# Delta rounds of a two-block transformer kernel: filler work dealt out anew between the levels

## The reference, cut to what matters

```python
h = rms_norm(x, g_mix)
glu_a, glu_b, q, k, v, z, a_in, b_in, gate_a, gate_b = split_cols(h @ w_in, IN_SIZES)
c = depthwise_conv(glu_a * sigmoid(glu_b), conv_dw_w) + conv_dw_b      # 31 taps, 1024 channels
c = silu(layer_norm(c, ...));  y_conv = c @ w_conv_out
qkv = silu(depthwise_conv([q, k, v], qkv_conv_w))                      # 5 taps
# gated delta rule, forward and backward in time, 8 heads of 128, chunked:
lower = strictly lower part of (k_beta @ k.T) * decay
sol = triangular_solve(lower, [v * beta, k_beta * exp(g)], unit_diagonal=True)
v_new = u - w @ state;  o = q_dec @ state + qk @ v_new
state = state * exp(g_last) + k_tail.T @ v_new
y = sigmoid(gate_a) * y_conv + sigmoid(gate_b) * (norm(o_fwd + o_bwd) * silu(z)) @ w_delta_out
pl = rms_norm(p @ w_pl_proj, g_pl_proj)                                # gated in later
```

## Time and profile before

| | us |
|---|---|
| median of 3 runs (lowest, highest) | 2165.98 (2165.07, 2167.03) |
| the profiled execution's own time | 2168.76 |
| its span, first to last instruction | 2167.0 |
| PE busy in it | 2105.1 (97%), 14346 matmuls |
| DVE, ACT, POOL busy | 1210.3, 853.3, 154.5 |
| mean granted TensorE clock | 0.995 |

### The profile page before, as it was taken

How to read it: one execution, slowest core, us unless ns; L and a number is a source line. 1 busy time by engine, 2 the same in 40 slices (tenths; PEclk the granted TensorE clock), 3 DMA queues, 4 the chain that set the end, 5 groups by cost and what they waited for, 6 DMA issues and landing times.

```text
span 2167.0 us, 35176 instructions
## 1 busy us (share of the span) xinstructions
PE 2105.1 (97%) x14346; PEld 1747.7 (81%) x14346; DVE 1210.3 (56%) x1888; ACT 853.3 (39%) x1400; POOL 154.5 (7%) x134
## 2 busy tenths in 40 slices
PE   6999999999999999999999999999999999999998
PEld 5878777787878888888888888888897688888887
DVE  4789888798645554444433644443247835444323
ACT  4344655346674333333223533332243544322222
POOL 0100021002421010000000100000000110000000
PEclk9999999999999999999999999999999999999999
DMA  4242111122012342233323233233212122333321
GB/s 166 81 134 80 60 46 50 60 78 65 31 63 87 127 159 88 97 97 97 120 94 107 69 90 96 96 101 111 98 59 62 37 69 79 96 96 97 116 94 53
DMA packets 56173, 189.95 MB, mean 88 GB/s; under 512 B 6256, under 2 KB 8688, under 8 KB 56048
## 3 DMA queue, kind: packets, MB, share of 16 engines
q1 hardware_dynamic: 53168, 182.92, 26.4%
q10 hardware_dynamic: 2880, 5.24, 0.6%
HBM read 178.70 MB, written 9.44 MB: 87 GB/s over the span
## 4 chain that ended last, share of the span: by engine, by line
PE 65%; DVE 3%; ACT 1%; issue 0%; POOL 0%; DVEq 0%; ACTq 0%
PE pg L716 61%; PE pC L820 1%; DVE w_lo L2021 1%; PE pA L794 0%; PE pC L794 0%; PE pB L778 0%; ACT w_hi L1393 0%; PE pB L747 0%; DVE a_lo L2080 0%; DVE sml L2680 0%; DVE sm L2678 0%; PE pA L754 0%; DVE mo L2717 0%; PE pC L1308 0%; ACT a_hi L1953 0%
## 5 line engine op out<-in xcount | busy, mean ns | idle before, releaser
L716 PE MATMUL pg<-a_hi,w_hi 128*128 128x512 f32 (+1 forms) x1920 | 747.4, 389 | 14.2 <-ACT ptile L1483 4.4
L716 PE MATMUL pg<-a_lo,w_hi 128*128 128x512 f32 (+1 forms) x1920 | 739.9, 385 | 0.0
L716 PE MATMUL pg<-a_hi,w_lo 128*128 128x512 f32 (+1 forms) x1920 | 737.9, 384 | 0.0
L2021 DVE TENSOR_TENSOR w_lo<-w_raw,w_hi 128x1024 fp32r<-128x1024 f32 (+3 forms) x299 | 386.3, 1292 | 386.7 <-ACT w_hi L1393 386.0
L1393 ACT ACTIVATE w_hi<-w_raw 128x1024 fp32r<-128x1024 f32 (+3 forms) x299 | 329.6, 1102 | 646.0 <-PE pg L716 635.4
L716 PEld LDWEIGHTS pg<-a_hi,w_hi 128*128 128x128 f32 x1920 | 362.3, 189 | 91.3 <-issue 9.2
L716 PEld LDWEIGHTS pg<-a_hi,w_lo 128*128 128x128 f32 x1920 | 361.9, 188 | 68.9 <-issue 1.4
L716 PEld LDWEIGHTS pg<-a_lo,w_hi 128*128 128x128 f32 x1920 | 362.3, 189 | 67.8 <-issue 0.9
L716 PE MATMUL pg<-h_hi,w_hi 128*128 128x512 f32 (+1 forms) x572 | 213.5, 373 | 0.5 <-DVE w_lo L2021 0.5
L716 PE MATMUL pg<-h_hi,w_lo 128*128 128x512 f32 (+1 forms) x572 | 213.3, 373 | 0.0
L716 PE MATMUL pg<-h_lo,w_hi 128*128 128x512 f32 (+1 forms) x572 | 213.2, 373 | 0.0
(11 more groups left out here) (397 smaller groups left out, 2216.7 us busy)
## 6 DMA issues: line engine op xcount, KB each, us to landing
w_raw<-in_w_gu SPq DMA_DIRECT2D x132, 512.0 KB, 3.5
w_raw<-in_w_in SPq DMA_DIRECT2D x74, 512.0 KB, 3.5
w_raw<-in_w_dn SPq DMA_DIRECT2D x48, 704.0 KB, 4.1
spill_g<-tmp ACTq DMA_DIRECT2D x16, 256.0 KB, 2.2
w_raw<-in_w_co SPq DMA_DIRECT2D x8, 512.0 KB, 3.9
w_raw<-in_w_do SPq DMA_DIRECT2D x8, 512.0 KB, 3.7
w_raw<-in_w_wo SPq DMA_DIRECT2D x8, 512.0 KB, 4.2
w_raw<-in_w_pg SPq DMA_DIRECT2D x8, 512.0 KB, 3.5
```

The lines of the kernel that those rows point to most:

```text
L716: ins = pe.matmul(dst[:, cols], w_of(w, n % 2, k), b(k)[:, cols], start=first and q == 0, stop=last and q == len(todo) - 1)
L2021: dve.tensor_tensor(w_lo[:, n % 2, 0:c], w_raw[:, n % 4, 0:c], w_hi[:, n % 2, 0:c].bitcast(F32), ALU.subtract).then_inc(S("w_lo"), 1)
```

## The change

It deals out the filler work of GLU, q, k, v and delta stages anew:

- The outputs `pl` 4 to 7 leave `pg` and its order; they go into `pA` and `pC`, which are free then.
- `TAPS` gets a new order: 8 taps of convolution 1 alone, then odd and even convolutions in turn, 8 of convolution 0 alone at the end; `CSUM` ends with 0. Doses: GLU 64 taps (56 before), q, k, v 56 (48), R = 0 25 (30), R = 1 to 3 26 each (30), R = 4 25 (24). In R = 1 to 3 one tap stands between L2358 and L2366.
- In rounds of three filler units the splits stand at gaps 7, 14 and 15 (before: 3, 11 and 15), and `GAP3` moves two matmuls from gap 1 to gap 2.
- `TAIL`: 15 matmuls ahead of the last sums, 9 behind.
- r = 0: ACT makes `lc` first, then the copy of turned v, then `gate_out(TAIL)`.
- `far` holds in R = 5 from level 2 on and in R = 6 from level 4 on.

```diff
-            if t == 0:
-                O.add(("pl", 4), "A")
...
-        TAPS = [(t, j) for pair in ((1, 2), (3, 4), (5, 6), (0, 7)) for j in range(CK) for t in pair]
+        LEAD = 8
+        ODD = [(t, j) for t in (1, 3, 5, 7) for j in range(CK)]
+        EVEN = [(t, j) for t in (2, 4, 6, 0) for j in range(CK)]
+        TAPS = ODD[:LEAD] + [z for pair in zip(ODD[LEAD:], EVEN) for z in pair] + EVEN[-LEAD:]
         GLU_TAPS = (5, 6)
-        QKV_TAPS = (((0, 0, 0), (0, 5, 3), (0, 5, 3), (0, 5, 3)), ((2, 3, 3), (2, 2, 2), (0, 3, 2), (0, 3, 2)))
+        QKV_TAPS = (((0, 0, 2), (0, 5, 3), (0, 5, 3), (0, 5, 3)), ((3, 4, 4), (2, 3, 3), (1, 3, 2), (0, 3, 2)))
...
-        GAP3 = [14, 14, 2, 3, 3, 3, 3, 1, 3] + [3, 3] * 2 + [4, 5, 5]
-        TAP = [1, 2, 0] + [1, 2] * 2 + [1, 3, 1, 2, 1, 3] + [0, 10, 0]
-        TAP4 = [1, 2, 0] + [1, 1] * 4 + [1, 2] + [0, 10, 0]
+        GAP3 = [14, 12, 4, 3, 3, 3, 3, 1, 3] + [3, 3] * 2 + [4, 5, 5]
+        TAP = [0, 4, 0, 2, 1, 1, 1, 1, 0, 1, 0, 1, 0, 0, 13, 0]
+        TAP0 = [2, 2, 0, 2, 1, 1, 0, 0, 2, 1, 2, 1, 0, 0, 11, 0]
         NORM_AT = 14
+        TAIL_AT = 15
...
-        def far(R):
+        def far(R, lv):
-            return R not in (5, 6)
+            return lv >= {5: 2, 6: 4}.get(R, 0)
...
-                    dst = begin(("pl", 2 * i + q))
+                    dst = begin(("pl", 2 * i + q)) if i < 2 else p_bank(2 * i + q)
...
-                        unit(TAIL[half], part=(0, 9))
+                        unit(TAIL[half], part=(0, TAIL_AT))
...
-                if r == 0:
-                    gate_out(TAIL[half])
-                    turned_out(HH * (half + 1) - 1, 1)
...
                 act.activation(lc[hi_], en[hi_, :, hi_], ACT.Copy).then_inc(S("lc"), 1)
+                if r == 0:
+                    turned_out(HH * (half + 1) - 1, 1)
+                    gate_out(TAIL[half])
...
-                if g % 2 and g > 1:
+                if len(filler(R)) == 3:
+                    if g in (7, 14, 15):
+                        after(filler(R)[(7, 14, 15).index(g)])
+                elif g % 2 and g > 1:
...
                 if R < 5:
-                    taps((TAP4 if R == 4 else TAP)[g])
+                    taps((TAP if R % NC else TAP0)[g])
...
                 if r == 0:
                     head_factors(half)
+                elif R < 4:
+                    taps(1)
```

More of the change, by code:

```diff
@@ L372, in build @@
             O.add(("glb", t), "A")
-            if t == 0:
-                O.add(("pl", 4), "A")
-                O.add(("pl", 5), "A")
             O.add(("gla", t), "D")
-            if t == 0:
-                O.add(("pl", 6), "A")
-                O.add(("pl", 7), "A")
         O.add(("ab",), "D")
@@ L469, in added @@
             return "add" if nu else "add0"
-        TAPS = [(t, j) for pair in ((1, 2), (3, 4), (5, 6), (0, 7)) for j in range(CK) for t in pair]
+        LEAD = 8
+        ODD = [(t, j) for t in (1, 3, 5, 7) for j in range(CK)]
+        EVEN = [(t, j) for t in (2, 4, 6, 0) for j in range(CK)]
+        TAPS = ODD[:LEAD] + [z for pair in zip(ODD[LEAD:], EVEN) for z in pair] + EVEN[-LEAD:]
         GLU_TAPS = (5, 6)
-        QKV_TAPS = (((0, 0, 0), (0, 5, 3), (0, 5, 3), (0, 5, 3)), ((2, 3, 3), (2, 2, 2), (0, 3, 2), (0, 3, 2)))
+        QKV_TAPS = (((0, 0, 2), (0, 5, 3), (0, 5, 3), (0, 5, 3)), ((3, 4, 4), (2, 3, 3), (1, 3, 2), (0, 3, 2)))
         A_, B_ = 4, 4
         GAP = [16, 17, 4, A_, B_, A_, B_, 1, B_] + [A_, B_] * 2 + [6, 8, 8]
-        GAP3 = [14, 14, 2, 3, 3, 3, 3, 1, 3] + [3, 3] * 2 + [4, 5, 5]
-        TAP = [1, 2, 0] + [1, 2] * 2 + [1, 3, 1, 2, 1, 3] + [0, 10, 0]
-        TAP4 = [1, 2, 0] + [1, 1] * 4 + [1, 2] + [0, 10, 0]
+        GAP3 = [14, 12, 4, 3, 3, 3, 3, 1, 3] + [3, 3] * 2 + [4, 5, 5]
+        TAP = [0, 4, 0, 2, 1, 1, 1, 1, 0, 1, 0, 1, 0, 0, 13, 0]
+        TAP0 = [2, 2, 0, 2, 1, 1, 0, 0, 2, 1, 2, 1, 0, 0, 11, 0]
         PD = 4
         NORM_AT = 14
+        TAIL_AT = 15
         UNIT = 3 * KT
         assert sum(GAP) == 4 * UNIT and sum(GAP3) == 3 * UNIT and \
-            4 * GLU_TAPS[0] + 6 * GLU_TAPS[1] + sum(sum(z) for q in QKV_TAPS for z in q) + 4 * sum(TAP) + sum(TAP4) >= len(TAPS)
-        CSUM = (1, 2, 3, 4, 5, 6, 0, 7)
+            LEAD + 4 * GLU_TAPS[0] + 6 * GLU_TAPS[1] + sum(sum(z) for q in QKV_TAPS for z in q) + 3 * (sum(TAP) + 1) + \
+            2 * sum(TAP0) >= len(TAPS)
+        CSUM = (1, 2, 3, 4, 5, 6, 7, 0)
         def cslot(t):
@@ L558, in bank, with p_bank @@
             return pg[:, O.at[key] % 2, :]
+        def p_bank(t):
+            return (pA, pC)[t // 2 - 2][:, t % 2 * HH:t % 2 * HH + HH, :].rearrange("p j c -> p (j c)")
         def onb(h):
@@ L666, in _ @@
                 if n == U.at[("ab",)]:
-                    sp.wait_ge(S("plf"), KT)
+                    sp.wait_ge(S("plf"), 4 + KT)
                     sp.dma_start(spill_p.rearrange("t p n -> p t n"), ptile[:]).then_inc(S("spp"), 16)
@@ L975, in qkv @@
                     if hh == HH:
-                        unit(TAIL[half], part=(9, UNIT))
+                        unit(TAIL[half], part=(TAIL_AT, UNIT))
             def gap(R, g):
@@ L1016, in turned_products @@
                         for s, b in (halves, halves[::-1])[:1 if lv == LEVELS - 1 else 2]:
-                            dst = ctr_far[b, hh, :] if far(R) and j >= HH else ctr[s, j, :]
+                            dst = ctr_far[b, hh, :] if far(R, lv) and j >= HH else ctr[s, j, :]
                             ins = pe.matmul(only(dst), yb[s, j, :], only(tb[s, j, :]), start=True, stop=True)
@@ L1482, in evac_p @@
                 for t in (2 * i, 2 * i + 1):
-                    act.activation(ptile[:, t], bank(("pl", t)), ACT.Copy).then_inc(S("evA"), 1)
+                    if i < 2:
+                        act.activation(ptile[:, t], bank(("pl", t)), ACT.Copy).then_inc(S("evA"), 1)
+                    else:
+                        act.activation(ptile[:, t], p_bank(t), ACT.Copy).then_inc(S("plf"), 1)
             def high_x(t):
@@ L1507, in _ @@
                     if t == 0:
-                        ev_wait(act, ("pl", 5))
+                        act.wait_ge(S("plf"), 2)
                     square(1, 2 * t, ptile[:, 2 * t])
@@ L1515, in _ @@
                     evac_p(3)
-                    ev_wait(act, ("pl", KT - 1))
+                    act.wait_ge(S("plf"), 4)
                 if t < 4:
@@ L2143, in _ @@
                     taps(GLU_TAPS[0])
+                if t == 2:
+                    taps(LEAD - LEAD // 2)
                 if t == 6:
@@ L2160, in _ @@
                     taps(GLU_TAPS[1])
+                if t == 1:
+                    taps(LEAD // 2)
             unit_out(dve, ("ab",))
@@ L2388, in delta @@
                     s = slice(0, P) if lv < LEVELS - 1 else lo_
-                    if far(R):
+                    if far(R, lv):
                         y = grown_dir(tb[s, 0:HH], lv, 0)
```

## The result

| | us |
|---|---|
| before, on the same chip: median of 4 (lowest, highest) | 2166.51 (2165.07, 2170.09) |
| after: median of 4 (lowest, highest) | 2154.85 (2153.95, 2156.09) |
| ratio, 95% interval | 0.9938 [0.9926, 0.9950] |
| the profiled execution: own time, span | 2156.09, 2154.3 |

What follows compares the result with a forecast made beforehand. PE was taken to bound the kernel, except where DVE's list in a level is longer. Gains less costs summed to 24.5 us: 2168.8 to 2144.3 profiled, 2141.5 for the median, range 2134 to 2153.

Steps and rivals of the forecast that it cites:

- banks: GLU stage: PE's three waits for ACT to free a bank of pg vanish; gain 5.4 us, bounds 0 to 5.6.
- levels: R=0 to 3: DVE's lists become shorter than PE's time; gain 4.1 us in each of R=1 to 3, 1.4 in R=0.
- clock in R=2 and 3: With L1117's wait gone, the stretches at granted clock 0.50 vanish; gain 3.05 us per round, 6.1 together.
- End of a round: DVE's split and 13 taps fit behind the last tb; only R=4's lone last 8 taps cost 0.45 us.
- rival D: DVE's block at the round's end overruns at 1.22 us a tap, 27 in all: 2168.2 or worse; 3%.
- the rule that was weighed for two taps of 0.9: Level at 328.08: exclusive VectorE/GpSimd port lock would make each of two taps wait; sum 0.9 us worse.
- clock behind the bank of r = 0: PE idles 3.5 us for ACT's bank; clock charge 1.0 in R=0, 0.5 in R=4, 0 to 3.4 each.
- far: R=5 and 6: turned products take 0.65 instead of 1.10 in six levels; gain 2.3 us, bounds 0.5 to 2.7.
- taps in q, k, v: Two more taps in the first stage cost nothing, six in the second cost 1.3 us, between 0 and 4.1.
- TAIL: Wait before L926 and slow clock behind it vanish, but PE waits at the Gram products instead; worth 0, bounds 1.7.
- The table load: ACT at r=0: costs 1.28 us; the skill's extra drain of 1.38, left out, would make the sum 2.8 worse.
- A: Levels still wait and the clock still falls, through taps beside POOL or ACT's copies: gain 12.3, 2153.7 us; 20%.

Runs made afterwards that it cites:

- E7: Kernel before with only the small outputs' banks changed (pA and pC, order of the small units): 2159.88, ratio 0.9970 to the kernel before.
- E12: Kernel before, unchanged, profiled again: 2171.00 in one run; the kernel before beside it 2167.58.
- E6: Kernel before with the taps of convolutions 7 and 0 one convolution after the other, POOL's sums in that order: 2174.38, ratio 1.0032 to the kernel before.
- E8: Kernel after with R=1 to 3's splits and taps as before, except 5 taps behind the last level: 2172.58, ratio 1.0009 to the kernel before.
- E1: Kernel after with taps of convolutions 7 and 0 in turn to the end, those of 1 and 2 alone early: 2147.88, ratio 0.9907 to the kernel before.
- E5: Kernel after with taps in turn to the end, plus two filler matmuls and two taps moved later at r=0: 2141.85, ratio 0.9880 to the kernel before.
- E9: Kernel after with E5's edits, plus ACT's masked copies of lc moved behind its level 3 copy: 2140.95, ratio 0.9875 to the kernel before.
- E11: Kernel after with TAIL split after 9 matmuls again instead of 15: 2154.07, ratio 0.9941 to the kernel before.
- E2: Kernel after with POOL's seven convolution sums held back until the last tap, tap order kept: 2147.22, ratio 0.9900 to the kernel before.
- E10: Kernel after with the near form of the turned products in all levels of R=5 and 6 again: 2155.96, ratio 0.9951 to the kernel before.
- E4: Kernel after with two filler matmuls moved behind the first products at r=0 and two taps to gaps 6 and 7: 2148.10, ratio 0.9909 to the kernel before.

## Why the prediction was right or wrong

**Right: banks.** 5.4 forecast, 5.5 in the trace of E7.

**Right: levels.** With the clock up on both sides, a round went from 48.3 (R=1) and 48.8 (R=2 in E7) to 44.5 and 44.6: 3.8 and 4.2, forecast 4.1. L1120 waits for nobody, L1106 still a little for et, as said.

**Right as a sum, loose as a term: clock in R=2 and 3.** The 6.1 fits the two profiles compared, but it isn't a fixed cost of the waits. Of 15 rounds R=1 to 3 with the old waits (before, E12, E6, E7, E8), 8 contain a stretch at 0.50; of 27 with the new levels (after, E1 to E5, E9 to E11), none.

**Wrong: "End of a round".** The step charged 0.45 for R=4, on the ground that the last 8 taps wait for each other, at 0.1 each. That much is true (0.12 in E2). It left out who else works there: POOL's sums, which in the kernel before also stood beside the taps, but were kept out by them, as its timeline has it:

```profile
533.10 8.03 DVE L2101 SCALAR_TENSOR_TENSOR cpad<-cpad,vec 128x512 f32<-128x512 f32 x12
534.62 7.68 POOL L2843 TENSOR_TENSOR acc<-cacc 128x512 f32<-128x512 f32 x1
```

The forecast itself had the row of a contended tap, 1.22, and used it in rival D as a price for all 13 taps of each round, at 3%, "against: 13 taps in 8.69". That 8.69 is of taps in turn; for a lone convolution it is no evidence. What it cost: 5.0 in R=4 and 3.2 of clock in R=5, 8.2 by trace, 7.0 in the medians, against 0.45.

The Trainium skill (SBUF — State Buffer, SBUF: two separate sides) has the rule that was weighed for two taps of 0.9 and should have been weighed here: the shared ports go to one of VectorE and GpSimd for a whole instruction. By that rule, a DVE that pauses between instructions lets POOL in each time, for the whole of a sum. The trace agrees: tap and sum by turns, six times, from the first pause of 0.04 on. Both a closed door (E1) and an absent POOL (E2) cure it; that the pause itself, and not something else about a chain, opens the door is read from this order of events and wasn't tried apart.

**Wrong: clock behind the bank of r = 0.** The wait came as forecast (3.5 in R=0 forecast, 3.27 measured). Charged were 1.0 and 0.5 for the clock, with a bound of 3.4 each; where the clock fell it took 2.5 in R=0 (E10 against the kernel after) and 1.7 in R=4 (from R=4's start to PE's wait for ACT's copy at level 3 it is 26.4 in E5, with a stretch, and 24.6 in E4, without). It fell in ten of the twelve such rounds of the six profiles with the old gaps. The forecast also took it as settled that PE must wait here, since two matmuls of the second unit stand ahead of L989, and netted it against what POOL gives back. Where they stand was a choice, and E4 moves them: with the taps that it moves as well, 3.8 and 3.9 less in these rounds.

**far, taps in q, k, v, TAIL.** far is worth about 2.4 by trace (forecast 2.3, bounds 0.5 to 2.7). R=3 with the second q, k, v lasts 133.54 in E7, where no stretch at 0.50 falls into it, and 130.15 after: 3.4 less, against 4.1 less 1.3 by the forecast. TAIL is worth 0 as far as the runs can tell.

**The table load.** All the rows show is 1.28 (222.12) with the sigmoid right behind it at 223.41, as before. The further drain of 1.38 that the Trainium skill (ScalarE: Activation LUTs, What ACT_TABLE_LOAD costs) states shows in none of the traces here behind a load whose next instruction waits for no other engine; leaving it out of the sum was right.

**Of the rivals**, A named the right total (2153.7) with the wrong cause: levels and clock in R=1 to 3 went as planned. D was right in its mechanism, and at the end of R=4 only.

## What to carry to other kernels

Before an order of independent steps is changed on an engine, ask which other engine works beside it at that place: VectorE's instructions in turn ran at 0.67 with GpSimd kept out, the same ones in a chain at 0.79 alone and at some 1.6 with GpSimd beside them. A result handed over earlier helps only if nothing in the receiver's queue ahead of its use needs what was put later in exchange; look at the receiver's next two instructions. And when a profile shows the clock down behind a wait, compare a second profile of the same kernel before the stretch is entered as a term: here it was there in about half of the rounds.

## What the runs showed of the hardware

- VectorE and GpSimd, both on 128x512 f32 with two inputs in SBUF: eleven taps back to back take 7.37 and stretch GpSimd's one sum to 7.87. In a chain each tap from the first pause on lets one sum through, and eleven take 13.22. In these runs who is kept out went with whether VectorE pauses between its instructions.
- Granted clock: the same instructions with the same waits had the clock down in R=2 and R=3 in one execution, in R=1 and R=2 in another, and each stretch costs R=2 up to 3.1 (51.88 for 48.79). In this kernel all such stretches of R=1 to 3 came with waits of 1.5 and more lost before L1117, though not each such wait had one.
- A stretch at 0.50 can cost nearly nothing for the round that it falls into: in E5 it lay ahead of a wait for another engine, and R=0 was as long as without it in E4 (46.45 and 46.47).
